# Expert turns written out, token rows gathered and added back by indirect DMAs

## What is computed

```python
logits = jnp.einsum('bsd,de->bse', x, w_router, preferred_element_type=jnp.float32)
top_val, top_idx = lax.top_k(logits, TOP_K)                      # TOP_K = 2
top_w = jax.nn.softmax(top_val, axis=-1)
combine = jnp.sum(jax.nn.one_hot(top_idx, N_EXPERTS) * top_w[..., None], axis=-2)
for e in range(N_EXPERTS):                                       # 8
    out = out + combine[..., e:e + 1] * swiglu(x, w_gate_up[e], w_down[e])
```

## Time and profile before

| | us |
|---|---|
| median of 3 runs | 1588.8 |
| lowest and highest | 1583.62, 1589.86 |
| span of the profiled execution | 1575.7 |
| busy in it: PE, DVE, ACT, POOL | 1505.1, 1203.9, 982.2, 149.2 |

### The profile page before, as it was taken

One profiled execution on the slowest core, in us unless ns is written; L12 is line 12 of the kernel. 1 busy time (PEld: TensorE's weight loads), 2 busy tenths in 40 slices (PEclk: granted clock), 3 DMA queues, 4 the chain that ended last, 5 costly groups with the idle time before them and its releaser, 6 DMA issues.

```text
span 1575.7 us, 19513 instructions
## 1 busy us (share of the span) xinstructions
PE 1505.1 (96%) x6965; PEld 1231.8 (78%) x6965; DVE 1203.9 (76%) x969; ACT 982.2 (62%) x835; POOL 149.2 (9%) x121
## 2 busy tenths in 40 slices
PE   6999999999998599999999999999999999999997
PEld 5777788887866488878878888887887887887885
DVE  5566555535675679889889889989979988988987
ACT  5445344433443277677777777767768767777774
POOL 3200000000300220020020002002002002002000
PEclk9989999999968799999999999999999999999998
DMA  9612365554420279999999999999999999999992
GB/s 356 215 54 94 121 187 187 186 187 146 175 81 21 73 255 360 358 331 357 369 325 354 370 329 343 365 344 343 358 355 335 362 356 329 363 356 334 358 359 94
DMA packets 194229, 427.22 MB, mean 271 GB/s; under 512 B 9184, under 2 KB 32016, under 8 KB 194192
## 3 DMA queue, kind: packets, MB, share of 16 engines
q1 hardware_dynamic: 191008, 423.68, 76.2%
q0 software_dynamic: 720, 2.62, 0.5%
q10 hardware_dynamic: 2464, 0.43, 0.2%
HBM read 425.65 MB, written 1.05 MB: 271 GB/s over the span
## 4 chain that ended last, share of the span: by engine, by line
PE 89%; DVE 4%; issue 2%; ACT 2%; POOL 1%; DMA 0%; ACTq 0%; DVEq 0%; POOLq 0%
PE ps L385 26%; PE ps L387 26%; PE ps L386 26%; PE ps L664 2%; PE ps L739 2%; ACT w_hi L765 1%; PE ps L442 1%; DVE w_lo L1011 1%; PE ps L556 1%; POOL head_r L1474 1%; PE ps L516 1%; PE ps L518 1%; PE ps L540 1%; PE ps L527 0%; DVE nat L1024 0%
## 5 line engine op out<-in xcount | busy, mean ns | idle before, releaser
L1011 DVE TENSOR_TENSOR w_lo<-raw,w_hi 128x2048 fp32r<-128x2048 f32 x404 | 936.3, 2330 | 239.8 <-ACT w_hi L765 238.7
L765 ACT CAST w_hi<-raw 128x2048 fp32r<-128x2048 f32 x404 | 771.0, 1912 | 342.6 <-PE ps L387 338.9
L385 PE MATMUL ps<-w_hi,t_hi 128*128 128x512 f32 x1328 | 531.2, 400 | 8.8 <-DVE w_lo L1011 5.3
L387 PE MATMUL ps<-w_lo,t_hi 128*128 128x512 f32 x1328 | 521.5, 393 | 0.0
L386 PE MATMUL ps<-w_hi,t_lo 128*128 128x512 f32 x1328 | 521.0, 392 | 0.0
L385 PEld LDWEIGHTS ps<-w_hi,t_hi 128*128 128x128 f32 x1328 | 251.9, 190 | 64.1 <-DVE w_lo L1011 7.9
L387 PEld LDWEIGHTS ps<-w_lo,t_hi 128*128 128x128 f32 x1328 | 251.3, 189 | 54.0
L386 PEld LDWEIGHTS ps<-w_hi,t_lo 128*128 128x128 f32 x1328 | 252.2, 190 | 49.6
L385 PE MATMUL ps<-w_hi,e_hi 128*128 128x512 f32 x448 | 179.5, 401 | 0.0
L387 PE MATMUL ps<-w_lo,e_hi 128*128 128x512 f32 x448 | 177.3, 396 | 0.0
L386 PE MATMUL ps<-w_hi,e_lo 128*128 128x512 f32 x448 | 177.2, 395 | 0.0
(11 more groups left out here) (227 smaller groups left out, 1011.6 us busy)
## 6 DMA issues: line engine op xcount, KB each, us to landing
raw<-in_moe_w_gate_up SPq DMA_DIRECT2D x224, 1024.0 KB, 6.7
raw<-in_moe_w_down SPq DMA_DIRECT2D x112, 1024.0 KB, 7.3
raw<-in_dense_w_gate_up SPq DMA_DIRECT2D x44, 512.0 KB, 4.7
raw<-in_w_in SPq DMA_DIRECT2D x20, 1024.0 KB, 6.2
raw<-in_dense_w_down SPq DMA_DIRECT2D x11, 1024.0 KB, 4.8
raw<-in_w_out SPq DMA_DIRECT2D x8, 1024.0 KB, 4.8
raw<-in_w_mem_kv SPq DMA_DIRECT2D x4, 1024.0 KB, 5.5
x<-in_x SPq DMA_DIRECT2D x2, 512.0 KB, 3.7
```

The costliest lines, as they stand in the source:

```text
L385: pe.matmul(dst, hi, w_hi[:, slot, c0:c0 + cn], start=first, stop=False)
L387: return pe.matmul(dst, hi, w_lo[:, slot, c0:c0 + cn], start=False, stop=last)
L765: act.copy(w_hi[:, n % SPLIT_SLOTS, :], raw[:, n % RAW_SLOTS, :]).then_inc(hi_ready, 1)
L1011: dve.tensor_tensor(w_lo[:, n % SPLIT_SLOTS, :], raw[:, n % RAW_SLOTS, :], w_hi[:, n % SPLIT_SLOTS, :].bitcast(F32), ALU.subtract).then_in ...
```

## The change

The first `STATIC` = 7 turns are written out on PE, ACT, DVE and POOL, turns 7 and up stay a loop of the same body; SP writes out all 8. Lines of the changed kernel are some 14 lower in the later engines' parts.

**Rows in.** POOL stores the normed rows to `tok` in HBM and stores `x` to `out`. During turn 0 POOL makes one-hot matrices for all 11 possible turns, PE multiplies each with a pair (token number, weight), 11 times two float32 matmuls of 2 columns, behind blocks 2, 4, ... 22, and DVE copies the results to `slot_i` and `slot_w`. From then on POOL fetches the 128 rows of the turn after the present one by an indirect DMA into `rows_of`; PE transposes them (8 transposes in fills of 4, 2 and 2, behind blocks 32, 35 and 38); ACT copies the high part, DVE subtracts. Slots that no token of the expert takes hold other tokens, with weight 0. Only turn 0 is still gathered by a one-hot product, now in float32 with `nat` and `pick0` (16 matmuls, no parts `n_hi`, `n_lo`).

**Rows out.** At block 2 of the next turn ACT scales `OUT` and DVE scales `OUT + 1` into `y`, and POOL adds `y`'s 128 rows to `out` in HBM by an indirect DMA that accumulates. PE waits for `y` (`y_ready`) only at the first down block. The two POOL additions, the scatter products, `pick_t`, `y_hi` and `y_lo` are gone. The number of turns is read on PE, ACT and DVE after turn 2 instead of before turn 0.

```diff
-            pe.wait_ge(nat_read, TILES)
-            pe.wait_ge(pick_ready, 1)
-            for f in range(4):
-                gather(f, spare(FILL[("gather", f)]))
-            for f in (0, 1):
-                taken(pe, FILL[("gather", f)])
-            pe.wait_ge(table_ready, 1)
-            turns = pe.value_load(table_i[0:1, 0:1], min_val=E, max_val=E + MAX_EXTRA)
-            with pe.Fori(0, turns) as i:
+            pe.wait_ge(pick0_ready, 1)
+            for f in range(2):
+                bank = spare(FILL[("gather", f)])
                 for j in range(4):
+                    k = 4 * f + j
                     for t in range(TILES):
+                        mm = pe.matmul(bank[:, j * P:(j + 1) * P], nat[:, t, k * P:(k + 1) * P], pick0[:, t, :],
                                        start=(t == 0), stop=(t == TILES - 1))
                 mm.then_inc(fill_ready, 1)
...
+                    if b == GU_BLOCKS:
+                        if first:
+                            pe.wait_ge(slots_taken, 2)
+                        else:
+                            for h in range(2):
+                                pe.wait_ge(y_ready[h], i)
...
-                    for f in range(4):
-                        if b == SCATTER_AT[f]:
-                            scatter(f, turn_spare(SCATTER + f), i * 2)
-                    if b == SLOTS_AT:
-                        bank = turn_spare(SLOTS)
+                    if first and b in SLOT_AT:
+                        c = SLOT_AT.index(b)
+                        pe.wait_ge(pick_ready, c + 1)
                         for t in range(TILES):
-                            pe.transpose(bank[:, t * P:(t + 1) * P], pick[:, t, :].bitcast(F32), ident[:])
-                        for t in range(TILES):
-                            mm = pe.matmul(bank[:, 2 * P:2 * P + 1], pick[:, t, :].bitcast(F32), turn_cw[:, t:t + 1],
+                            mm = pe.matmul(ps[:, OUT, 2 * c:2 * c + 2], pick[:, c % 2, t, :], turn_iw[:, t, c, :],
                                            start=(t == 0), stop=(t == TILES - 1))
...
-                    if b in GATHER_AT:
-                        f = GATHER_AT.index(b)
+                    if b in ROWS_AT:
+                        f = ROWS_AT.index(b)
+                        bank = turn_spare(ROWS + f)
                         if f == 0:
-                            pe.wait_ge(pick_ready, i + 2)
-                        gather(f, turn_spare(GATHER + f))
+                            pe.wait_ge(rows_landed, i * 16 + 16)
+                        for j, k in enumerate(range(*ROWS_OF[f])):
+                            mm = pe.transpose(bank[:, j * P:(j + 1) * P], rows_of[:, k * P:(k + 1) * P], ident[:])
+                        mm.then_inc(fill_ready, 1)
+            for i in range(STATIC):
+                turn(i)
+                if i == LOAD_TURNS_AT:
+                    pe.wait_ge(table_ready, 1)
+                    turns = pe.value_load(table_i[0:1, 0:1], min_val=E, max_val=TURNS)
+            with pe.Fori(STATIC, turns) as i:
+                turn(i)
```

POOL, in place of its loop of additions:

```diff
+            for t in range(TILES):
+                pool.wait_ge(nat_ready, 4 * TILES + t + 1)
+                pool.dma_start(tok[t * P:(t + 1) * P, :], nat[:, t, :]).then_inc(tok_stored, 16)
+            for t in range(TILES):
+                pool.dma_start(out[0, t * P:(t + 1) * P, :], x[:, t, :]).then_inc(added, 16)
...
+            def gather(rows):
+                pool.indirect_dma_start(out=rows_of[:], out_offset=None, in_=tok,
+                                        in_offset=bass.IndirectOffsetOnAxis(ap=rows, axis=0)).then_inc(rows_landed, 16)
+            def scatter(n, rows):
+                for h in range(2):
+                    pool.wait_ge(y_ready[h], n)
...
+                pool.indirect_dma_start(out=out[0], out_offset=bass.IndirectOffsetOnAxis(ap=rows, axis=0), in_=y[:], in_offset=None,
+                                        compute_op=ALU.add).then_inc(added, 16)
...
+            for i in range(STATIC):
+                if i:
+                    pool.wait_ge(fill_ready, i * TURN_FILLS + FILL_MOE)
+                gather(slot_i[:, i + 1:i + 2])
+                if i:
+                    pool.wait_ge(added, i * 16 + 16)
+                    scatter(i, slot_i[:, i - 1:i])
...
+            scatter(turns, cur_i[:, 1:2])
+            pool.wait_ge(added, turns * 16 + 32)
```

More of the change, by code:

```diff
@@ L1406, in _, with take_y @@
[L1406 to L1410 removed]
+            split_to(BLK_MOE + SPLIT_SLOTS)
+            def take_y(i, factor):
+                dve.wait_ge(w_used, i * TURN_BLOCKS + BLK_MOE)
+                dve.wait_ge(added, i * 16 + 16)
+                dve.tensor_scalar(y[:, BANK:D], ps[:, OUT + 1, :], factor, None, ALU.mult).then_inc(y_ready[1], 1)
@@ L1418, in _ @@
                 for b in range(TURN_BLOCKS):
+                    if not (first and b == 0):
+                        split(BLK_MOE + b + SPLIT_SLOTS - 1, i)
+                    if b == 2 and not first:
+                        take_y(i, factor)
                     if b % 4 == 3 and b < GU_BLOCKS:
@@ L1461, in _ @@
+            with dve.Fori(STATIC, turns) as i:
+                dve.wait_ge(turn_set, i)
+                turn(i, cur_w[:])
+            dve.wait_ge(turn_set, turns)
+            take_y(turns, cur_w[:])
         @block.gpsimd
@@ new lines, in _ @@
+            pool.wait_ge(slots_taken, 2)
+            pool.wait_ge(tok_stored, 16 * TILES)
+            pool.wait_ge(added, 16 * TILES)
+            for i in range(STATIC):
+                if i:
[4 more added lines that the diff above has]
+                    scatter(i, slot_i[:, i - 1:i])
+                    pool.memset(turn_mark[:, i:i + 1], 1.0).then_inc(turn_set, 1)
```

309 lines of the change are left out of this document (147 added, 162 removed).

## The result

The changed kernel takes 1520.6 us in the median of 4 runs (1520.3 to 1525.8), beside 1586.2 us for the kernel before in the same rounds: a ratio of 0.960, with a 95% interval of 0.957 to 0.963. The forecast was 1542 us, with 1528 to 1572 as its range. It is faster, as forecast, and by 21 us more than forecast.

A forecast was written before the change was run, and what follows sets the result against it. PE's issue was taken to bound the turns while loads keep up. Seven turns -39.1, turn 0 0, ahead -3, behind -5, reading the number of turns +0.5: -46.6 from 1588.8 gives 1542 us, range 1528 to 1572.

The forecast's parts named there:

- What bounds it: Expert turns: a turn's length is the sum of what PE issues, as long as the weight loads keep up.
- The turn's term, -5.6: Turns 1 to 7: PE work removed less transposes added, -6.1 us, with +0.5 for late loads; seven turns give -39.1.
- allowance of 0.5 us for late loads: Each turn: loads expected at their edge, with an odd late block, +0.5 us a turn.
- The slots: PE in each turn: 1.5 us removed, most of it a wait for ACT's copies of the scatter.
- Turn 0, 0: First turn: small float32 products +4.9, PE's -6.1 and about +1 for POOL's comparisons beside DVE, so no change.
- Ahead of the turns, -3: Before the first turn: second norm -2.0, memset and cast -2.3, float32 gather +1.5; net -3, between -5 and 0.
- The float32 gather: First gather, ahead of the turns: 16 float32 products cost 8.2 us where 32 before cost about 6.7, +1.5.
- Behind the last turn, -5: Program end: one scaling, then an accumulating indirect DMA taken at 6 us; about -5, between -7.5 and -3.
- Rivals 1 and 2: Loads bound the turns: mildly, 1562 or 1551 us, chance 0.18; or added rows make it slower, 1619 us, chance 0.08.
- Rival 3: Seven written-out turns stall PE in code loading, up to 13 us more, 1555 us; chance 0.06.
- Rival 4: POOL's indirect DMAs are slow, rows landing after block 32 or y free late; 1552 us if turn 0 alone; chance 0.06.
- The base: Whole kernel: the sum was applied to 1588.8 us, the median of runs shown, 13.1 us above the 1575.7 us span.

The follow-up runs named there:

- h1: Kernel before with an early Silu ahead of the loop and an unused 192-byte tile, putting e_hi 128 bytes beyond a multiple of 256: 1566.1 us, ratio 0.989.
- f2: Changed kernel with an unused tile of 64 bytes a partition ahead of the tiles that stages share: 1538.1 us, ratio 0.972.
- h5: Changed kernel with the indirect DMAs of turns 1 to 6 replaced by DMAs of 64 bytes: 1520.9 us.
- h6: Changed kernel with one more load of 0.79 MB in each of turns 1 to 7: 1521.1 us.
- f4: Kernel before with one more ACT instruction, a Silu of 4 columns, ahead of the loop of turns: 1569.6 us, ratio 0.992.
- i1: Changed kernel, unchanged, measured again in the same rounds as the repeat of the further version: 1520.0 us, ratio 0.958.
- h2: Changed kernel with turn 0's slot products two blocks later and ACT scaling both halves of y behind the last turn: 1515.8 us, ratio 0.958.
- h3: Changed kernel with its scatters as plain writes that overwrite rows and do not add: 1517.9 us.
- h4: Changed kernel with eight more loads of 0.79 MB in each of turns 1 to 7: 1600.9 us.
- f3: Changed kernel with three turns written out and the others in the loop, turn_mark kept at 11 columns so tiles stay in place: 1519.1 us.
- e0: Kernel before, measured again with no edit: 1588.7 us, ratio 1.001.
- i2: Repeat of the changed kernel with slot products two blocks later and ACT scaling both halves behind the last turn: 1515.5 us, ratio 0.956.
- e1: Kernel before with n_hi and n_lo placed ahead of e_hi and e_lo in SBUF: 1580.5 us, ratio 0.998.
- e2: Kernel before with its first 7 turns written out on PE, ACT, DVE and POOL: 1576.9 us, ratio 0.996.
- f1: Kernel before with an unused tile of 64 bytes a partition ahead of the tiles that stages share: 1579.7 us, ratio 0.999.

## Why the prediction was right and wrong

**What bounds it: right.** A turn is what PE issues. With 5.4 us of PE's work gone a turn is 5.4 us shorter (h1 against the changed kernel), with PE busy in all of it. Of the signs named for it these came: PE busy all through, no gather or scatter products in turns 1 to 7, 377 to 386 GB/s, ACT's waits on PE, DVE at 106.5 us. Two did not: a turn of 120 to 120.5 us (118.6) and an end 9 us behind the last product (11.8).

**The turn's term, -5.6, was -7.4.** This is the step that failed, 12.4 us, where the whole sum missed 11.7 (the other terms nearly cancel). It has three parts.
- The step took it, without a reason, that the products which stay keep their pace. Those of the down blocks went from 0.233 to 0.227 us, 168 in a turn, since `e_hi` and `e_lo` came to lie elsewhere: 0.8 to 1.0 us a turn by h1 and f2. The rows for it were read, 0.227 beside 0.235 (the latter with the longer product behind a fill in it), and passed over; a diff that adds small tiles ahead of large ones moves the large ones, and this was not looked at. That the tiles of the changed kernel fell on the quick place was luck, some 7 us over the eight turns, and nothing that the change aimed at.
- The allowance of 0.5 us for late loads was for nothing: h5 and h6 show a turn that doesn't notice 1.6 MB less or 0.8 MB more.
- The rest, some 0.3 us, is in the pieces. The removed ones took 6.8 us as forecast, the added transposes 0.64 for 0.7; the product behind a fill takes 0.06 to 0.09 us longer than the others, and with seven such fills gone for three new ones that is 0.2, which the sum left out.

The slots were priced rightly at 1.5 us and explained only halfway. Most of it was a wait for ACT's copies, as said; that the copies were late because of a table load in every turn, and that one instruction would have mended it in the kernel before (f4, 1.2 us a turn), the forecast didn't see. It names the reloads among what ACT loses and gives them no price.

**Turn 0, 0, was +1.9.** The slot products cost what was said (0.45 each, 4.9). The +1 for POOL's comparisons was the mis-sized term: the first ones come too late for block 2, 1.95 us, and the clock that falls behind this wait takes another 1.4. The place of the tiles gives 0.9 back. Two more things, which the forecast did not name, go against each other. Before, the first seven products of the turns still ran at the half clock, 1.5 us in all, and in i1 the clock is back before them. And PE now waits for DVE's split of the third block, 0.9 us with the slower products behind it:

```profile
552.85 0.50 PE L387 MATMUL ps<-w_hi,t_hi 128*128 128x512 f32 x1 [0.66 <-DVE w_lo L1003]
```

h2, which takes the wait away and leaves the comparisons, is 3.7 us shorter in this turn.

**Ahead of the turns, -3, was -6.3.** The norm (1.28 in place of 3.30) and the memset and cast came as said, -2.0 and -2.3. The float32 gather was the mis-sized term: +1.5 forecast, -0.8 measured (6.07 us in i1, 5.65 in the first profile, where the 32 before took 6.86). The windows of the two gathers, before and i1:

```profile
545.92:552.78 6.86, 6.86 (x32) 6.86 (x33) 2.97 (x18) 2.05 (x4) 0.00 (x0) 0.50 0.02 4
```

```profile
540.41:546.48 6.07, 6.07 (x33) 6.07 (x33) 1.62 (x7) 0.59 (x1) 0.00 (x0) 0.57 0.02 4
```

The larger part, 1.4 us, is the price. At the half clock 16 products in float32 were to take 8.2 us; each of them is two records, and in the stretch at half clock the records start 0.213 us apart, as the 32 float32r products before do, so 16 products take 6.8. The 0.257 us each that was read from the earlier trace rows at full clock has the step to another kind of product in it; within the group the records are 0.112 apart, 0.223 a product. The other 0.8 is the clock, which rises within the gather, to 0.57 and 0.63 on the mean where it was 0.50; the text had put an earlier rise at the edge of its range, -5, not in the middle. Of the remaining 1.2 us, 1.0 is one more operation that the sum left out: before, ACT copied the first `n_hi` (1.06 us from 525.3) ahead of the second norm's sum of squares, which starts 1.0 us earlier in i1.

**Behind the last turn, -5, was -2.3.** Taken were 6 us from the scaled result to the end; it is 9.2 in i1. The DMA's own time came out as taken, 6.0 us from issue to landing, its adding 2.6 of it by h3. Put at nothing were what stands on both sides of it: 0.9 us on POOL ahead of the issue (its mark and the issue), and 2.3 from the landing to the end. Of these 1.9 are a DRAIN instruction of POOL, which starts 0.2 us behind the landing; before, SP stored the result, its own drain took 0.01 us, and 0.4 us lay between the landing and the end. The Trainium skill ("DMA: Bandwidth & Descriptors", Anatomy of one DMA) gives a fixed part and one by bytes, which come to an estimate of 3.2 us; the plain write in h3, alone, took 3.4, which agrees, and the adding one 6.0.

**The rivals.** Rivals 1 and 2 did not come, by a margin now known, 384 GB/s needed and 394 to be had. The 357 and 375 GB/s on which they rested were no ceilings. In both PE was busy nearly throughout (17.62 and 18.00 of 18 us), so neither shows what the DMA engines could give. The Trainium skill ("DMA: Bandwidth & Descriptors", Specifications) has its 358 GB/s for a core as half of what the two cores on a stack share, and by it the result would have been 1593 us. This kernel runs on one core, and its turns, with those of h6 and h4, ran at 377 to 394 GB/s, so the figure is no limit for it; what the neighbouring core did is in no trace. Rival 3 (code written out stalls): the changed kernel with 7 and with 3 turns written out has the same turn (f3). Rival 4 (slow indirect DMAs): 6 to 11 us, with 16.8 us or more to spare in the two profiles of the changed kernel. All four ends on the side of a longer time were given weight, 0.38 in sum, while nothing stood on the shorter side below 1528; the one unknown that could be seen in the rows, the two paces of the same product, was no case at all.

**The base.** The sum was set against 1588.8, the median of the runs shown, and read the 13.1 us between it and the span as time around the span. In one and the same execution that is 2.0 to 2.1 us (e0: 1589.7 and 1587.6); the rest was a quick draw ahead of the turns, set against a median of slow ones. In the rounds of the result the median before was 1586.2, which is 2.6 us of the miss. By stretches the change is worth 58.3 us; by medians 65.6 here and 69.4 in i1's rounds. The difference lies ahead of the turns, where nothing was changed but places. Of the ten profiles with the tiles at 128, eight reach DVE's last addition to `x` by 522.5 to 524.9 us, the other two at 529.7 and 530.1; of the eight with another place one does (523.5, the profile that the forecast used) and seven come at 526.7 to 535.4. The medians are 524.4 and 530.0. The dense layer's down products, with 264 of the same kind of stationary tiles, explain 1.7 of these 5.6 us (60.2 us in place of 61.9 from the first to the last). Whether places weigh on the draw of the clock in 450 to 520 us is not shown. For it speaks f2, which is 17.5 us above the changed kernel where its eight turns account for 8 and the dense layer for 1.7. Against it speak the timed runs: within 5 us of their own fastest lie 17 of 24 runs of the kernels at 128 (the changed one twice, h1, h2 and i2), and 26 of 40 of e1, e2, f1 and f4, at other places, but only 21 of 68 of the kernel before. So what makes its median slow stays open; the one profile of it that was at hand was a quick draw.

## What to carry to other kernels

Where PE sets the pace, price each piece as distances between the starts of matmuls, and ask of every product that stays whether its operands still begin where they did: a small tile put ahead of large ones changed the pace of a third of the products by 3%, which was an eighth of the gain of a turn. Read the median of a row of DMAs as what it is, and the last DMA by itself. At the end of the program ask which engine comes last: here POOL's drain took 1.9 us that SP's did not. Look in a loop for what straight-line code would not do, here two function-table loads a turn, which one instruction ahead of the loop takes away. A short wait on PE costs its length and then the lower clock behind it; move what it waits for before moving anything else.

## What the hardware showed that was not expected

- The pace of 128-column stationary tiles against 512 columns depends on where they begin in a partition: 0.227 us at 128 bytes beyond a multiple of 256, 0.233 at 0, 96 and 192 beyond.
- A wait of 1.95 us in the midst of full work was followed by some 4 us at about the pace of the half clock (granted clock 0.82 to 0.86 in the windows there), and both were gone in h2.
- An indirect DMA with 128 rows of 4 KB lands in 6.0 to 6.3 us when it is alone and adds, in 3.4 when it overwrites (h3), and in 6 to 11 among weight loads; POOL itself spends 1.6 to 2.8 us on the adding one. A DRAIN on POOL behind the last landing takes 1.9 us (i1), 2.1 in h3.
- Loads of 1 MB from HBM into SBUF ran at 394 GB/s for 130 us at a time on one core, and the busy share of the DMA engines read 1.04 at 386 GB/s (i1), where no load was waited for, as it did at 394.
